# Four plain gate and up pairs in place of six, with GpSimd adding squares and forming quadrant sums, in a float32 hybrid encoder block

## What is computed

```
x1  = x + rmsnorm(mixer(x))                    # residual after the mixer
h   = rmsnorm(x1)                              # needs the sum of squares of x1 over all channels
g   = conv3(h @ w_gate) ;  u = h @ w_up        # w_gate, w_up: 2048 x 6144
y   = (gelu(g) * u) @ w_down
out = x1 + rmsnorm(y)
```

## Time and profile before

| what | value |
|---|---|
| median of 3 runs | 2223.37 us (2223.24 to 2224.24) |
| the profiled execution's own time | 2222.32 us |
| its span in the profile | 2220.7 us |
| TensorE matmul busy | 2183.4 us, 98% |
| TensorE weight loads busy | 1928.7 us, 87% |
| VectorE, ScalarE, GpSimd busy | 1530.0, 1002.6, 140.6 us |
| granted TensorE clock, mean | 0.995 |

### The profile page before, as it was taken

How to read it: one execution, slowest core, us unless ns; L and a number is a source line. 1 busy time by engine, 2 the same in 40 slices (tenths; PEclk the granted TensorE clock), 3 DMA queues, 4 the chain that set the end, 5 groups by cost and what they waited for, 6 DMA issues and landing times.

```text
span 2220.7 us, 34413 instructions
## 1 busy us (share of the span) xinstructions
PE 2183.4 (98%) x13320; PEld 1928.7 (87%) x13320; DVE 1530.0 (69%) x2021; ACT 1002.6 (45%) x1274; POOL 140.6 (6%) x207
## 2 busy tenths in 40 slices
PE   7999999999999899999999999999999999999998
PEld 5788888887788688999999999999998888888886
DVE  7677776777855777888888888888885444444445
ACT  5555554457322454444444444444444343343433
POOL 0000000000100000111111111111102000000000
PEclk9999999999999899999999999999999999999999
DMA  5232222222432436777777777777768322323343
GB/s 171 79 93 83 97 87 97 97 91 79 132 124 95 142 109 181 211 208 204 211 207 209 211 212 211 204 202 204 212 179 293 123 95 95 96 98 98 101 165 114
DMA packets 99853, 328.67 MB, mean 148 GB/s; under 512 B 12944, under 2 KB 20240, under 8 KB 99616
## 3 DMA queue, kind: packets, MB, share of 16 engines
q1 hardware_dynamic: 75200, 240.59, 32.1%
q0 software_dynamic: 22240, 82.36, 17.0%
q10 hardware_dynamic: 2304, 4.20, 0.5%
HBM read 306.09 MB, written 21.00 MB: 147 GB/s over the span
## 4 chain that ended last, share of the span: by engine, by line
PE 91%; DVE 5%; issue 2%; ACT 1%; DMA 1%; POOL 0%; SPq 0%; DVEq 0%; ACTq 0%; POOLq 0%
PE bank L1676 29%; PE bank L1677 29%; PE bank L1678 29%; DVE w_all L996 1%; PE bank L1735 1%; PE bank L1748 1%; DMA raw<-weights 1%; ACT w_all L557 1%; DVE x_b L1667 0%; DVE act_lo L1332 0%; PE bank L1760 0%; PE bank L1759 0%; DVE act_lo L1011 0%; DVE xc L1185 0%; PE bank L1706 0%
## 5 line engine op out<-in xcount | busy, mean ns | idle before, releaser
L1676 PE MATMUL bank<-act_hi,w_all 128*128 128x512 f32 (+1 forms) x1760 | 620.0, 352 | 19.7 <-DVE act_lo L1011 14.2
L1678 PE MATMUL bank<-act_hi,w_all 128*128 128x512 f32 (+1 forms) x1760 | 614.3, 349 | 0.0
L1677 PE MATMUL bank<-act_lo,w_all 128*128 128x512 f32 (+1 forms) x1760 | 612.4, 348 | 0.0
L1676 PEld LDWEIGHTS bank<-act_hi,w_all 128*128 128x128 f32 x1760 | 332.1, 189 | 67.9 <-issue 20.1
L1678 PEld LDWEIGHTS bank<-act_hi,w_all 128*128 128x128 f32 x1760 | 331.8, 189 | 46.7
L1677 PEld LDWEIGHTS bank<-act_lo,w_all 128*128 128x128 f32 x1760 | 332.0, 189 | 44.1 <-issue 0.2
L1006 DVE TENSOR_TENSOR w_all<-raw,w_all 128x1024 fp32r<-128x1024 f32 x96 | 117.7, 1226 | 286.8 <-ACT w_all L563 286.8
L1677 PE MATMUL bank<-w_all,act_hi 128*128 128x512 f32 x768 | 302.3, 394 | 0.0
L1676 PE MATMUL bank<-w_all,act_hi 128*128 128x512 f32 x768 | 301.0, 392 | 1.2 <-DVE w_all L1006 1.2
L1678 PE MATMUL bank<-w_all,act_lo 128*128 128x512 f32 x768 | 298.7, 389 | 0.0
L996 DVE TENSOR_TENSOR w_all<-raw,w_all 128x1024 fp32r<-128x1024 f32 x136 | 166.5, 1224 | 156.6 <-ACT w_all L557 154.8
(11 more groups left out here) (264 smaller groups left out, 3659.5 us busy)
## 6 DMA issues: line engine op xcount, KB each, us to landing
raw<-weights SPq DMA_DIRECT2D x310, 512.0 KB, 3.5
raw_s<-weights SPq DMA_DIRECT2D x84, 512.0 KB, 4.7
raw_s<-weights POOLq DMA_DIRECT2D x84, 512.0 KB, 6.0
raw_a<-weights SPq DMA_DIRECT2D x42, 512.0 KB, 5.0
h_spill<-h_out POOLq DMA_DIRECT2D x48, 256.0 KB, 3.6
h_t<-h_spill POOLq DMA_DIRECT2D x24, 512.0 KB, 7.2
x<-xT POOLq DMA_DIRECT2D x16, 256.0 KB, 3.1
out<-x ACTq DMA_DIRECT2D x16, 256.0 KB, 2.2
```

Source lines behind the costliest of these rows:

```text
L1676: pe.matmul(dst, ah, bh, start=start, stop=False, skip_group_check=goes_on)
L1677: pe.matmul(dst, ah, bl, start=False, stop=False, skip_group_check=goes_on)
L1678: return pe.matmul(dst, al, bh, start=False, stop=stop, skip_group_check=goes_on)
```

## The change

Two of the plain pairs become fast pairs (PLAIN 6 to 4, so 44 fast pairs). The 15 adds of squares go from VectorE to GpSimd, and so does `t_form`, now four plain adds or subtracts, each step into its own place in `t_raw`, which is the memory of the low halves of `tsum`. One of the four sums is formed with the opposite sign and turned by ScalarE (`scale=-1.0`) and VectorE. `x1_sum` moves ahead of unit 8. Units 14 and 15 are split into the third slot and slot 0. The cores of the diff:

```diff
-PLAIN = 6
+PLAIN = 4
+        t_raw = sb_in(sums, "t_raw", [4, 2, UK, HS])      # same place as tsum
-            k = (q + 2) % 3
+            k = (q + 1) % 3
 # GpSimd
-            for j in range(PLAIN - 2):
-                store_h(j)
+            chain = Chain(pool, pool_chain)
+            for k in range(1, KT):
+                pool.wait_ge(x1sq_done, k + 1)
+                ins = pool.tensor_tensor(acc[:], og[:, 0] if k == 1 else acc[:], og[:, k], ALU.add)
+                chain(ins) if k < KT - 1 else ins.then_inc(x1sum_ready, 1)
+            def t_form(k):
+                pool.wait_ge(x1_gained, k + 1)
...
+                t0, t1, t2, t3 = [t_raw[:, t, 1, k] for t in range(4)]
+                pool.tensor_tensor(t2, b22, b12, ALU.subtract)
+                chain(pool.tensor_tensor(t1, b11, b12, ALU.subtract))
+                chain(pool.tensor_tensor(t0, b22, t1, ALU.add))
+                pool.tensor_tensor(t3, t0, b21, ALU.subtract).then_inc(t_formed, 1)
+            for k in range(UK):
+                t_form(k)
+                if k == 4:
+                    store_h(0)
+                elif k == 6:
+                    store_h(1)
 # ScalarE: t_hi, then the new order of the list
+                act.activation(tsum[:, 0, 0, k], t_raw[:, 0, 1, k], ACT.Copy, scale=-1.0)
+                act.activation(tsum[:, 1:4, 0, k], t_raw[:, 1:4, 1, k], ACT.Copy).then_inc(t_hi_done, 1)
...
             gain_x1(0)
             gain_x1(1)
+            split(N_FF + 9, 1)
+            root(5, SB[2], std)
             gain_x1(2)
             gain_x1(3)
+            t_hi(0)
+            split(N_FF + 10, 0)
             gain_x1(4)
+            t_hi(1)
             last_tap(0)
             gain_x1(5)
+            t_hi(2)
+            split(N_FF + 11, 1)
+            gelu_gate(0)
+            gain_x1(6)
+            t_hi(3)
+            last_tap(1)
+            gain_x1(7)
+            t_hi(4)
+            split(N_FF + 12, 0)
+            gelu_gate(1)
+            t_hi(5)
+            last_tap(2)
             split(N_FF + 13, 1)
+            t_hi(6)
             gelu_gate(2)
             t_hi(7)
+            split(N_FF + 14, 0, to=w_slot(-2)[0])
+            split(N_FF + 15, 1, to=w_slot(-1)[0])
+            last_tap(PLAIN - 1)
             product_hi(0, 0)
+            gelu_gate(PLAIN - 1)
             product_hi(0, 1)
 # VectorE: t_lo, then the new order
+                dve.scalar_tensor_tensor(out=tsum[:, 0, 1, k], in0=t_raw[:, 0, 1, k], scalar=-1.0,
+                                         in1=word(tsum[:, 0, 0, k]), op0=ALU.mult, op1=ALU.subtract)
+                dve.tensor_tensor(tsum[:, 1:4, 1, k], t_raw[:, 1:4, 1, k], word(tsum[:, 1:4, 0, k]),
+                                  ALU.subtract).then_inc(t_split, 1)
...
+  split 8, split 9, reciprocal, gate_in(0), t_lo(0), split 10, taps(0), t_lo(1), t_lo(2), split 11,
+  up_tile(0), gate_in(1), t_lo(3), taps(1), t_lo(4), split 12, up_tile(1), gate_in(2), t_lo(5),
+  taps(2), split 13, t_lo(6), split 14, up_tile(2), t_lo(7), split 15, gate_in(3), form_s2(0),
+  product_lo(0,0), taps(3), product_lo(0,1), product_lo(0,2), up_tile(3)
 # TensorE
+            x1_sum()
             tile(N_FF + 8, PJ[0])
-            tile(N_FF + 10, PJ[1], between=x1_sum)
+            tile(N_FF + 10, PJ[1])
...
+            unit(N_FF + 14, 2, 0, SB[2], True, False)
+            unit(N_FF + 15, 0, 1, SB[2], False, True)
-            pe.wait_ge(t_split, UK)
...
                 fast_product(i, 0, a, quadrant(0, 0), True)
...
+                if not i:
+                    pe.wait_ge(t_split, UK)
                 fast_product(i, 1, b, t_sum(0), True)
```

More of the change, by code:

```diff
@@ L234, in block_kernel @@
         outp.close()
+        sums = ExitStack()
+        t_raw = sb_in(sums, "t_raw", [4, 2, UK, HS])
+        sums.close()
         ffn = ExitStack()
@@ L279, in block_kernel @@
             x1_back_landed lifted taken
-            stored dve_chain""".split()
+            stored dve_chain pool_chain""".split()
         (par_landed, hi_done, split_done, unit_used, consts_set, zeros_set,
@@ L297, in block_kernel @@
          eps_y_done, x1_back_landed, lifted, taken,
-         stored, dve_chain) = [sem(n) for n in names]
+         stored, dve_chain, pool_chain) = [sem(n) for n in names]
         x_landed = [sem(f"x_landed{c}") for c in range(len(X_CHUNKS))]
@@ L552, in _, with split @@
         def _(act):
-            def split(u, s, more=MORE):
+            def split(u, s, more=MORE, to=None):
                 act.wait_ge(raw_landed[s], (u - s) * 8 + (16 + more[s]))
                 at_least(act, unit_used, u - 1)
-                act.activation(w_hi[s], raw[:, s], ACT.Copy).then_inc(hi_done, 1)
+                act.activation(to or w_hi[s], raw[:, s], ACT.Copy).then_inc(hi_done, 1)
             def split_down(n, s):
@@ L920, in _ @@
                 product_hi(i, 4)
-                gelu_gate(j - 1)
+                if i:
+                    gelu_gate(j - 1)
                 product_hi(i, 5)
@@ L991, in _, with split @@
             chain = Chain(dve, dve_chain)
-            def split(u, s):
+            def split(u, s, slot=None):
+                hi, lo = slot or (w_hi[s], w_lo[s])
                 dve.wait_ge(hi_done, u + 1)
-                dve.tensor_tensor(w_lo[s], raw[:, s], word(w_hi[s]), ALU.subtract).then_inc(split_done, 1)
+                dve.tensor_tensor(lo, raw[:, s], word(hi), ALU.subtract).then_inc(split_done, 1)
             def split_h(n, s, ku):
@@ L1449, in up_tile @@
                 dve.tensor_tensor(h_out[:, j % 2], bank[:], cv[:], ALU.mult).then_inc(h_done, 1)
[L1451 to L1456, removed]
-            split(N_FF + 8, 0)
[L1459 to L1480, removed]
+            split(N_FF + 8, 0)
             def t_lo(k):
                 dve.wait_ge(t_hi_done, k + 1)
-                dve.tensor_tensor(tsum[:, :, 1, k], t_f32, word(tsum[:, :, 0, k]), ALU.subtract).then_inc(t_split, 1)
+                dve.scalar_tensor_tensor(out=tsum[:, 0, 1, k], in0=t_raw[:, 0, 1, k], scalar=-1.0,
+                                         in1=word(tsum[:, 0, 0, k]), op0=ALU.mult, op1=ALU.subtract)
+                dve.tensor_tensor(tsum[:, 1:4, 1, k], t_raw[:, 1:4, 1, k], word(tsum[:, 1:4, 0, k]),
+                                  ALU.subtract).then_inc(t_split, 1)
             def open_used(j, part):
                 return N_FF + (OPEN if j < 2 else 4 * j + 2 + 2 * part)
-            split(N_FF + 11, 1)
+            split(N_FF + 9, 1)
             invert_root(5, rms[:], std, 4)
@@ L1493, in _ @@
             chain(dve.memset(gb[:, 0:2], 0.0))
-            split(N_FF + 12, 0)
             gate_in(0, SB[0], open_used(0, 0))
+            t_lo(0)
+            split(N_FF + 10, 0)
             taps(0)
-            split(N_FF + 13, 1)
+            t_lo(1)
+            t_lo(2)
+            split(N_FF + 11, 1)
             up_tile(0, SB[1], open_used(0, 1))
             gate_in(1, PT[0], open_used(1, 0))
-            t_form(0)
+            t_lo(3)
             taps(1)
-            split(N_FF + 14, 0)
+            t_lo(4)
+            split(N_FF + 12, 0)
             up_tile(1, PT[1], open_used(1, 1))
             gate_in(2, PJ[0], open_used(2, 0))
-            t_lo(0)
+            t_lo(5)
             taps(2)
-            split(N_FF + 15, 1)
+            split(N_FF + 13, 1)
+            t_lo(6)
+            split(N_FF + 14, 0, w_slot(-2))
             up_tile(2, PJ[1], open_used(2, 1))
[L1509 to L1534, removed]
             t_lo(7)
-            split(N_FF + 23, 1)
+            split(N_FF + 15, 1, w_slot(-1))
             def product_lo(i, n):
@@ L1585, in _ @@
                     taps(j - 1)
+                else:
+                    up_tile(PLAIN - 1, SB[2], N_FAST)
                 product_lo(i, 3)
@@ L1593, in _ @@
                     fast_h(j - 1, i - 1)
-                else:
-                    up_tile(PLAIN - 1, PT[1], N_FAST)
                 product_lo(i, 5)
@@ L1680, in w_tile @@
             def w_tile(s, c):
-                return w_hi[s][:, c * P:c * P + P], w_lo[s][:, c * P:c * P + P]
+                hi, lo = (w_hi[s], w_lo[s]) if s < 2 else (w_2[:, 0], w_2[:, 1])
+                return hi[:, c * P:c * P + P], lo[:, c * P:c * P + P]
             def unit(u, s, half, bank, start, stop, each=None, middle=None):
```

54 lines of the change are left out of this document (7 added, 47 removed).

## The result

The changed kernel takes 2234.59 us (median of 5 runs, 2232.8 to 2235.65) against 2223.37 before: ratio 1.0049, interval 1.0035 to 1.0064. The forecast was 2218.2. The range held the time; the direction was wrong, and what came is what rival 1 described. The profiled execution took 2234.20 us, with a span of 2232.5.

A forecast was written before the change was run, and what follows sets the result against it. The prediction took TensorE's own pace as the bound, with room on VectorE and ScalarE. Terms -5.85 + 0.5 + 0.2 gave -5.15 us, so 2218.2 us against the median; the range was 2217.0 to 2236.

The forecast's parts named there:

- rival 1: Opening and plain units: GpSimd reads hold back VectorE's two-SBUF-input instructions; +7 us, about 2230, up to 2236; chance 0.31.
- TensorE's work: Two plain pairs go (43.95 us), two fast pairs come (38.10 us, 19.05 each): gain 5.85 us.
- Squares on GpSimd: Opening: adds at 1.4 us keep pace with squares every 2.75 us, sum complete at 778.9, slack 4.3 us; cost nothing.
- `t_form` on GpSimd: Plain units: eight steps of four 0.7 us instructions, step 7 ending at 811.6, slack 3 us before unit 14; cost nothing.
- Lists: ScalarE's and VectorE's instruction order before unit 12: weight split done 807.4, unit due 806.94; wait 0.5 us, up to 1.5.
- Hand-over: Start of the fast pairs: product 1's operands ready at 832.2, wanted at 832.1; wait 0.2 us, upper end 3.
- Sum: Whole kernel: -5.85 + 0.5 + 0.2 = -5.15 us, forecast 2218.2 us against the median.
- Rival 2: Late wait before unit 14 (3 to 4 us) or product 1 (2 to 3) takes most gain: 2222 or 2221; chance 0.26.

The follow-up runs named there:

- e4: The kernel before, with 15 extra GpSimd adds of two square tiles into a scratch tile nobody reads: 2231.45 us, ratio 1.0036.
- e2: The changed kernel with only GpSimd's 15 adds replaced by pairs of memsets, quadrant sums still reading: 2223.55 us, ratio 1.0001.
- e1: The changed kernel with GpSimd's adds and quadrant operations all replaced by pairs of memsets, so it reads nothing: 2216.77 us, ratio 0.9972.
- e3: The changed kernel with only the 32 GpSimd quadrant operations replaced by pairs of memsets, adds still reading: 2225.38 us, ratio 1.0008.
- e7: Against the kernel before: five plain pairs, adds and quadrant sums on VectorE, sums in the change's places, GpSimd computing nothing: 2218.09 us, ratio 0.9978.

## Why the prediction was wrong, step by step

- **TensorE's work, -5.85.** Right: no wait in the fast pairs, 19.05 us each, 44 of them.
- **Squares on GpSimd, cost nothing.** This is the first step that failed. Its price was right (1.33 alone against 1.4), its slack too: the sum was complete before `x1_sum` and nobody waited for GpSimd. What failed is "cost nothing": the cost fell on VectorE's instructions, which the step didn't look at. e4 measures it at 8.8 us. The step's side remark, about 2 us to pay at 2.8 us an add, doesn't follow from its own rows either: with squares every 2.75 us and the last at 777.4, such adds would end near 781, still ahead of 783.22. It didn't enter the sum.
- **`t_form` on GpSimd, cost nothing.** The second failed step, in the same way. Its price was right alone, 0.74 us an instruction against 0.7, but a collision makes it up to 1.73, and step 7 ended at 827.9 where 811.6 was forecast. No wait of TensorE hangs on that; the cost is VectorE's longer instructions, 7.3 us with the adds' reads gone (e2 against e1).
- **Lists, 0.5 us ahead of unit 12.** Right once the reads are gone: 0.67 us in e1.
- **Hand-over, 0.2 us.** No such wait in e1 or after; the range of this term went to 3.
- **Sum, -5.15.** e1 gives -5.14 for the stretch and 2216.77 us where the forecast stood at 2218.2. So the working was sound for a GpSimd that reads nothing, and the interference is nearly the whole error: 17.5 us of stretch between e1 and after. That the stretch agrees to 0.01 us is luck in part, since the pace of TensorE alone moves it by more. In the medians e1 is 6.3 us below the kernel before and not 5.15; the rest lies outside the stretch.
- **Rival 1.** The mechanism, place and sign came true. Its terms: 1.2 us a round over six rounds, less 0.8, were forecast for the opening; measured 1.76 a round over five rounds, 9.1 in all. I had let 0.61 us of each add lie beside L1411 for free; in the round shown neither add ran beside that instruction. After the opening 4 to 8 were forecast, and 9.4 came, of which 1.9 are TensorE's slow restart after a long wait and 0.5 are in the forecast itself. The 7 forecast as its sum were 11.2 in the medians.
- **Its chance, 0.31.** I weighed it down by "no row here shows it" and by the hope that an add might take 0.85 us. But its conditions were all in the rows: VectorE busy 5.1 of 5.49 us, and three of four instructions in the opening with both inputs in SBUF. The Trainium skill, SBUF — State Buffer, section Who interferes with whom, states the contention itself. That no row showed it was no evidence against it, since in the kernel before GpSimd does no arithmetic on data there, so no row could show it. More than half the chance belonged there. That the wide range held the time is no merit of the forecast: its upper end was put there for this rival.
- **Rival 2** did not come: the long wait is ahead of unit 12, by VectorE's own lateness, and goes away when the reads do.

## What to carry to other kernels

Before work is moved to GpSimd, ask not only whether GpSimd has time but which VectorE instructions run beside it. If these have both inputs in SBUF and VectorE is near its pace, price each GpSimd instruction twice: its own length, and a stall on VectorE. Here an add of 1.33 us held VectorE for about 1.1 us. The 32 instructions of 0.74 us lengthened VectorE's by 11.4 us together, an estimate from the groups of e2 and e3, some 0.36 each. VectorE's products with an input in PSUM and its reciprocal kept their lengths beside GpSimd's reads, and GpSimd's memsets cost nothing; other pairs were not measured. An engine with 9% of busy time can cost the kernel more than it relieves; look for it in the length of the neighbours' instructions, not in its own row.

## What the runs showed of the hardware

- A two-input GpSimd add of 128x512 takes 1.33 us, of 128x256 0.74. Beside a VectorE instruction with two SBUF inputs, the later of the two mostly does its work after the earlier, though the quadrant low half at 812.96 was held by two instructions that started behind it (0.42 became 2.11): 0.74 became 1.79, 1.23 became 2.31 on VectorE; 1.33 became 1.73 and 0.74 became 1.73 on GpSimd.
- A GpSimd copy of 128x512 (0.93 us) costs such a VectorE instruction only 0.36 to 0.40 us; a memset costs nothing. Why a copy costs so much less than an add wasn't found out.
- VectorE's reciprocal (3.34) and its products with PSUM (0.68 to 0.69) kept their lengths beside GpSimd's reads.
- TensorE restarted at the lower clock after idling 5.16 us (0.40 to 0.56 us a matmul, nine of them), and again in e2 after 5.19; it did not after idling 1.29 or 1.44.
- At a granted clock of 1.00 there are two paces, 0.2289 and 0.2333 us a 128x512 matmul, for stretches of some 10 to 60 us. In e7 it is 0.2333 from 744 to 794, in the kernel before from about 850 to 872. What sets them stays open.
